# One filler product on the identity put in at every second block of the router's logits

## The reference

```python
def moe_swiglu(h, router, w_gate, w_up, w_down):
    logits = (xt @ router).astype(jnp.float32)        # 256 x 1024 by 1024 x 8
    top_val, top_idx = lax.top_k(logits, TOP_K)
    gates = jax.nn.softmax(top_val, axis=-1)
    ...                                               # tokens sorted by expert
    def expert_block(args):
        tok, gt, e = args
        xb = x_pad[tok]
        hid = jax.nn.silu(xb @ w_gate[e]) * (xb @ w_up[e])
        return (hid @ w_down[e]) * gt[:, None]
```

## Time and profile before

| | |
|---|---|
| time, median of 3 runs | 1464.52 us |
| lowest and highest run | 1464.15 and 1466.93 us |
| span of the profiled execution | 1465.1 us |
| PE busy | 1454.8 us, 99% |
| DVE, ACT, POOL busy | 1197.8, 975.0, 123.3 us |
| DMA | 450.23 MB, 307 GB/s over the span |
| mean granted clock of PE | 0.993 |

### The profile page before, as it was taken

One profiled execution on the slowest core, in us unless ns is written; L12 is line 12 of the kernel. 1 busy time (PEld: TensorE's weight loads), 2 busy tenths in 40 slices (PEclk: granted clock), 3 DMA queues, 4 the chain that ended last, 5 costly groups with the idle time before them and its releaser, 6 DMA issues.

```text
span 1465.1 us, 20232 instructions
## 1 busy us (share of the span) xinstructions
PE 1454.8 (99%) x7509; PEld 1223.5 (84%) x7509; DVE 1197.8 (82%) x974; ACT 975.0 (67%) x894; POOL 123.3 (8%) x136
## 2 busy tenths in 40 slices
PE   9999999999999999999999999999999999999998
PEld 8978888888988888888888888888888888888886
DVE  5776766666886788888888888889888888888897
ACT  4465544445456477777777777777777777777775
POOL 5312000000222360000000000000000000000200
PEclk9999999999999899999999999999999999999999
DMA  8633985462533499999999999999999999999994
GB/s 253 227 116 117 348 282 201 156 209 82 173 115 116 149 398 396 393 381 394 376 370 395 373 369 395 388 359 391 391 369 373 395 382 370 394 381 353 399 394 171
DMA packets 210282, 450.23 MB, mean 307 GB/s; under 512 B 12940, under 2 KB 37048, under 8 KB 210232
## 3 DMA queue, kind: packets, MB, share of 16 engines
q1 hardware_dynamic: 208936, 445.09, 83.2%
q0 software_dynamic: 1152, 4.19, 0.7%
q10 hardware_dynamic: 144, 0.26, 0.0%
HBM read 435.36 MB, written 14.16 MB: 307 GB/s over the span
## 4 chain that ended last, share of the span: by engine, by line
PE 99%; ACT 0%; DVE 0%; POOL 0%; issue 0%; DVEq 0%; POOLq 0%
PE bank L1724 27%; PE bank L1726 26%; PE bank L1725 26%; PE bank L2172 5%; PE bank L2174 3%; PE bank L2221 2%; PE bank L1881 1%; PE bank L1731 1%; PE bank L2199 0%; PE bank L1921 0%; PE bank L1911 0%; PE bank L1950 0%; PE bank L2209 0%; PE bank L1744 0%; PE bank L1805 0%; PE bank L1812 0%
## 5 line engine op out<-in xcount | busy, mean ns | idle before, releaser
L1215 DVE TENSOR_TENSOR low<-raw,high 128x2048 fp32r<-128x2048 f32 x336 | 767.1, 2292 | 104.1 <-ACT high L1116 103.5
L1116 ACT CAST high<-raw 128x2048 fp32r<-128x2048 f32 x335 | 643.5, 1921 | 178.1 <-PE bank L1726 178.1
L1724 PE MATMUL bank<-high,xeh 128*128 128x512 f32 x896 | 353.5, 395 | 0.0
L1726 PE MATMUL bank<-high,xel 128*128 128x512 f32 x896 | 349.5, 390 | 0.0
L1725 PE MATMUL bank<-low,xeh 128*128 128x512 f32 x896 | 348.9, 389 | 0.0
L1726 PEld LDWEIGHTS bank<-high,xel 128*128 128x128 f32 x896 | 168.2, 188 | 35.8
L1725 PEld LDWEIGHTS bank<-low,xeh 128*128 128x128 f32 x896 | 168.4, 188 | 33.7
L1724 PEld LDWEIGHTS bank<-high,xeh 128*128 128x128 f32 x896 | 168.3, 188 | 33.5
L1724 PE MATMUL bank<-high,hdh 128*128 128x512 f32 x444 | 173.6, 391 | 0.0
L1726 PE MATMUL bank<-high,hdl 128*128 128x512 f32 x444 | 172.9, 389 | 0.0
L1725 PE MATMUL bank<-low,hdh 128*128 128x512 f32 x444 | 172.8, 389 | 0.0
(11 more groups left out here) (372 smaller groups left out, 1869.5 us busy)
## 6 DMA issues: line engine op xcount, KB each, us to landing
raw<-in_moe_w_gate_dram SPq DMA_DIRECT2D x112, 1024.0 KB, 7.5
raw<-in_moe_w_up_dram SPq DMA_DIRECT2D x112, 1024.0 KB, 8.2
raw<-in_moe_w_down_dram SPq DMA_DIRECT2D x112, 1024.0 KB, 7.9
ring<-in_w_in_dram SPq DMA_DIRECT2D x10, 2048.0 KB
dring<-in_dense_w_gate_dram SPq DMA_DIRECT2D x5, 2048.0 KB
dring<-in_dense_w_up_dram SPq DMA_DIRECT2D x5, 2048.0 KB
dring<-in_dense_w_down_dram SPq DMA_DIRECT2D x5, 2048.0 KB
ring<-in_w_in_dram SPq DMA_DIRECT2D x8, 1024.0 KB, 8.7
```

The source lines that it names most:

```text
L1116: act.copy(high[:, q % SPLIT, :], raw[:, q % RAW, :]).then_inc(s_hi, 1)
L1215: dve.tensor_tensor(low[:, q % SPLIT, :], raw[:, q % RAW, :], high[:, q % SPLIT, :].bitcast(F32), ALU.subtract).then_inc(s_lo, 1)
L1724: pe.matmul(o, xh, wh, start=first, stop=False)
L1726: return pe.matmul(o, xl, wh, start=False, stop=last)
```

## The change

After the blocks 0, 2, 4 and 6 of each call of `router_logits` one product of the identity with the identity, 128 columns wide and taken four times (512 columns), is done into bank 0. The bank is written anew, with its start flag, before it is next used.

```diff
@@ router_logits
                     ins = pe.matmul(ps[6][:, t * NE:(t + 1) * NE], hT[:, k, t * P:(t + 1) * P], RW[:, k, :],
                                     start=(k == 0), stop=(k == KD - 1))
+                    if k % 2 == 0:
+                        keep_running(0, 1)
                 if t == T - 1:
                     ins.then_inc(s_lg, 1)
```

## The result

The changed kernel takes 1468.6 us (median of 20 runs, 1465.5 to 1470.74) against 1465.45 us for the kernel before (20 runs, 1462.31 to 1468.45). The ratio is 1.0021, 95% interval [1.0014, 1.0027]: 3.1 us slower, from 2.0 to 4.0. That is just over the 2.9 us that had been named as the bound of what can be told; 1467.0 had been forecast, and 1463.9 to 1468.9 as the range.

What follows compares the result with a forecast made beforehand. PE bounds the kernel through a fixed-length expert stage; logits ending 3.56 us later, partly regained when the clock returns in the gather, give +2.5 us on 1464.5, so 1467.0 us, range 1463.9 to 1468.9.

Steps and rivals of the forecast that it cites:

- What bounds: Expert stage: a fixed length of PE work, so a shift of its first product goes one to one into the end.
- The fillers' price: Router logits: eight fillers on PE's path, 0.228 us each, 1.82 us at full clock.
- The fall: Router logits: clock still halves at about 495.80, five fillers done, so logits end 3.56 us later.
- the rival in which the clock falls late, in the gather: Gather partly at half clock, logits 1.6 us more: -0.5 to +0.9 us; chance 0.11 together with cheap fillers.
- cheap fillers: Logits: fillers lie wholly in weight loads, at least 0.9 us, 1465.4; chance 0.11 together with the late fall.
- its sign of being wrong: End of the logits: clock still 1.00 there, time then about as before or 1 us under.
- The full-clock rival: Clock stays full to the expert stage, DVE becomes the later one: -1.0 us, 1463.5; chance 0.13.
- The sum in the profile: Logits to expert stage: logits end and gather start 3.56 us later; expert stage +1.85 to +3.8, taken as +2.5.
- the middle case: Gather: clock returns 3.41 us in, gather ends at 508.79, expert stage starts 2.3 us later.
- late-return case: Gather: clock returns only 6 us in or not within it, +3.5 to +3.8 us, 1468.2; chance 0.18.
- The time: Whole kernel: +2.5 us on the timed median 1464.52, giving 1467.0; profiled span taken as 0.6 above that median.

Runs made afterwards that it cites:

- the third trace: Changed kernel unaltered, profiled in one more execution; one run, 1465.92 us.
- the second trace: Changed kernel unaltered, profiled in another execution; one run, 1468.32 us.
- The wide kernel with eight fillers: Changed kernel's eight fillers plus logit products widened from 8 to 128 columns; 1466.04 us, ratio 1.0009 to the kernel before.
- none behind: Kernel before without its four fillers behind the logits; 1465.82 us, ratio 1.0005.
- eight in front: Kernel before with eight fillers in one block ahead of the logits; 1467.64 us, ratio 1.0015 to the kernel before.
- first call only: The change in the first call of the logits alone, four fillers; 1467.84 us, ratio 1.0012 to the kernel before.

## Why the prediction was right

**What bounds.** What follows the first expert product, the expert stage to the end of the program, kept its length to 0.2 us while its start moved by over 6 us. Shown in all fourteen traces.

**The fillers' price.** 0.228 us was used; 0.227 measured at full clock, 1.83 us for eight in a pair of kernels without a fall. The 1.05 us that follows from the page "TensorE: Matmul & The Clock Gate" of the Trainium skill did not hold here.

**The fall.** It was expected at 495.80, 3.3 us into the logits. It came at 496.48, 3.7 us in, with six fillers started in place of five; in the third trace at 4.1 us. But the second trace is the rival in which the clock falls late, in the gather: one execution in three seen, of a case that had 0.11 together with cheap fillers. In that execution the clock was still full at the end of the logits, which the prediction had named as its sign of being wrong. Its stretch, 13.93 us, is that of both traces of the kernel before, within the -0.5 to +0.9 us that the rival had been given.

**The full-clock rival**, given 0.13, did not occur in the changed kernel's three traces, and its price was wrong. It was to make the kernel 1.0 us faster than before, with xel starting when DVE's job steps end. But xel starts only 1.12 us after the last job step has started, as DVE first reads the job count into a register. The wide kernel with eight fillers, which had no fall, took 14.00 us in place of the 13.0 that the rival amounts to: even then the eight fillers gain nothing on the 13.95 us of before.

**The sum in the profile.** L1589 was to be 3.56 us later; it is 3.44 later. The gather was to start 3.56 later; 503.48 is 3.45 later. The clock's return 3.41 us into the gather was the middle case, +2.3 us; it came 3.2 us in (506.72), and the stretch grew by 1.95. Time against time the two profiled executions differ by 2.3. One step of the late-return case was summed wrongly: a return 5.1 us into the gather gives +3.1 us by its own terms, not +2.9.

**The time.** The forecast was +2.5 us, measured are +3.1. The term that was mis-sized is the average over executions. The sum took the profiled execution of before, whose gather ran almost wholly at half clock, as the typical one, and set its difference on the median as if that run stood 0.6 us above it; it stood 2.4 above. Two traces without any early fall show what other executions look like (busy time by stretch: first the kernel with none behind, which differs from before only in the four fillers in the wait, then the changed one, third trace):

```profile
489.69:493.52 3.83, 3.71 (x32) 3.62 (x32) 2.92 (x4) 3.83 (x7) 1.30 (x3) 1.00 0.95 312
493.52:500.35 6.83, 5.29 (x24) 5.21 (x25) 5.32 (x27) 3.18 (x3) 1.19 (x3) 0.50 0.30 118
...
489.76:493.84 4.08, 4.08 (x31) 3.82 (x31) 2.84 (x3) 4.08 (x7) 1.30 (x3) 1.00 0.96 316
493.84:504.08 10.24, 10.24 (x44) 9.30 (x43) 5.42 (x27) 3.13 (x4) 1.52 (x5) 0.50 0.18 70
```

At full clock the logits take 3.7 us without fillers and 5.6 with eight. A fall 3.8 us in finds the first kernel done with them and a stretch of 12.48 us; 4.1 us in it finds the changed one with two fillers to come, and the stretch is 15.80. The two runs took 1462.63 and 1465.92 us, 3.3 apart, more than the fillers' 1.83. So fillers that lengthen the logits also give the fall more room to strike inside them. The times fit: a start of the logits at 489.7, the 958.6 us behind the stretch and the 1.8 us outside the span leave 12.2 us for the stretch of before's fastest run of 20 (1462.31), and 15.4 for the changed kernel's (1465.50).

How often each case occurs is not known from so few traces. A rough estimate goes by the clock over many runs: before had 0.9944 on average (the 35 runs of the first set of experiments), the changed kernel 0.9936 (20 runs). Among the 35, the medians by clock are 1466.8 us at 0.993 (4 runs), 1465.6 at 0.994 (18), 1464.3 at 0.995 (5), 1462.6 at 0.996 (7): some 1.4 us for 0.001. The changed kernel's 0.0008 is then 1.1 us, which with 1.83 us for the fillers gives 2.9 of the 3.1. These clocks also hold the early falls, so the split is worked out, not measured by itself. That the total came as near as 0.6 us is in part luck: the pair of stretches differs by 1.95, 1.85 or -0.02 us, depending on which trace of the changed kernel is taken.

**The late return**, given 0.18, was not seen: the latest came 4.0 us into the gather (third trace, 504.08).

## What to carry to other kernels

A filler that keeps the matrix engine's clock up must either stand where the engine waits anyway or stream more columns under weight loads that are there already; among products on the critical path it costs its own length, and too few of them don't hold the clock each time, so that some of that length is paid at half clock. When the clock is up, look for what is late next before counting the gain: here it was a vector engine's register read. And where the clock falls at another place in each execution, one trace is one sample; take the length of the pieces from traces and the verdict from many runs.

## What the runs showed of the hardware

- Widening a plain float32 product from 8 to 128 columns cost nothing: 0.111 us a pass against 0.113.
- With PE busy without a break, a stretch of narrow products brings the clock down (before: fall at 495.82 and 496.98; PE busy 3.27 of 3.30 us ahead of the first). It did not in every execution: in three traces with the same narrow products (none behind, eight in front, first call only) it fell only after the logits, at 493.52, 497.54 and 501.10, and in the second trace of the changed kernel in the gather. The stretches at half clock ahead of the expert stage lasted 3.41, 6.8 or 10.2 us.
- The vector engine started its next instruction 1.12 us behind the start of the last job count when it first read the count into a register, 0.18 us when it did not.
- Each early fall of 3.41 us, in the first layer or at 392 to 395 us, moved everything behind it by about 1.4 us, and the same program had from none to three of them.
